# SSD scan of a hybrid decoder step: ScalarE scales the sample states by their decay in place, VectorE adds the products for four batches in one operation

## The reference

```python
def step(s, inp):
    xc, dtc, bc, cc = inp
    acum = jnp.cumsum(dtc * a, axis=1)
    ...
    y_inter = jnp.einsum('bign,bghpn->bighp', cc, s) * jnp.exp(acum)[..., None]
    a_last = acum[:, -1]
    w = jnp.exp(a_last[:, None] - acum) * dtc
    s_new = jnp.exp(a_last)[..., None, None] * s + jnp.einsum('bjgh,bjghp,bjgn->bghpn', w, xc, bc)
```

## Time and profile before

| what | value |
|---|---|
| median of 3 runs | 2334.03 us (2333.56 to 2342.25) |
| the profiled execution | 2328.8 us |
| its span, first to last instruction | 2327.3 us |
| mean granted TensorE clock | 0.955 of full speed |
| PE busy in the span | 2131.6 us, 92% |
| DVE busy | 1436.1 us, 62% |
| ACT busy | 937.9 us, 40% |
| POOL busy | 279.8 us, 12% |
| the states' updates, L2035 on DVE | 256 operations, from 1410.0 to 2048.4 us of the span |

### The profile page before, as it was taken

How to read it: one execution, slowest core, us unless ns; L and a number is a source line. 1 busy time by engine, 2 the same in 40 slices (tenths; PEclk the granted TensorE clock), 3 DMA queues, 4 the chain that set the end, 5 groups by cost and what they waited for, 6 DMA issues and landing times. The chain is left out here.

```text
span 2327.3 us, 41668 instructions
## 1 busy us (share of the span) xinstructions
PE 2131.6 (92%) x15171; PEld 1983.0 (85%) x15171; DVE 1436.1 (62%) x2762; ACT 937.9 (40%) x1260; POOL 279.8 (12%) x423
## 2 busy tenths in 40 slices
PE   6699999999999999968999699999999999749997
PEld 4698989999999898938999698988988988639996
DVE  5553756648465574844434468878878888744433
ACT  3444444434444334313333344544544545423332
POOL 1100201012001010120000102122121131110000
PEclk8799999999999999978999799999999999869999
DMA  4664858577658485547444466566565566336542
GB/s 126 205 174 124 276 159 276 191 226 221 210 158 284 125 281 148 190 174 269 162 156 164 133 175 194 168 194 196 168 218 182 173 200 192 102 143 220 162 154 77
DMA packets 332531, 427.42 MB, mean 184 GB/s; under 512 B 17132, under 2 KB 296220, under 8 KB 330976
## 3 DMA queue, kind: packets, MB, share of 16 engines
q1 hardware_dynamic: 293488, 287.16, 41.0%
q0 software_dynamic: 38720, 138.84, 16.8%
q10 hardware_dynamic: 224, 0.05, 0.0%
HBM read 350.63 MB, written 75.34 MB: 183 GB/s over the span
## 5 line engine op out<-in xcount | busy, mean ns | idle before, releaser
L132 DVE TENSOR_TENSOR w_lo<-w_raw,w_hi 128x1024 fp32r<-128x1024 f32 x512 | 624.9, 1225 | 651.5 <-ACT w_hi L126 641.4
L126 ACT ACTIVATE w_hi<-w_raw 128x1024 fp32r<-128x1024 f32 x512 | 541.4, 1060 | 1017.3 <-PE bank L147 950.4
L145 PE MATMUL bank<-xn_hi,w_hi 128*128 128x288 f32 x3072 | 927.9, 302 | 24.4 <-ACTq L931 12.3
L146 PE MATMUL bank<-xn_lo,w_hi 128*128 128x288 f32 x3072 | 911.7, 297 | 0.0
L147 PE MATMUL bank<-xn_hi,w_lo 128*128 128x288 f32 x3072 | 909.1, 296 | 0.0
L145 PEld LDWEIGHTS bank<-xn_hi,w_hi 128*128 128x128 f32 x3072 | 581.9, 189 | 47.5 <-issue 31.3
L146 PEld LDWEIGHTS bank<-xn_lo,w_hi 128*128 128x128 f32 x3072 | 582.7, 190 | 4.9
L147 PEld LDWEIGHTS bank<-xn_hi,w_lo 128*128 128x128 f32 x3072 | 583.3, 190 | 0.0
L145 PE MATMUL bank<-oc_o_hi,w_hi 128*128 128x288 f32 x512 | 153.9, 301 | 22.9 <-DVE oc_o_lo L1386 21.2
L145 PE MATMUL bank<-oa_o_hi,w_hi 128*128 128x288 f32 x512 | 154.5, 302 | 21.4 <-DVE oa_o_lo L1386 18.5
L146 PE MATMUL bank<-oa_o_lo,w_hi 128*128 128x288 f32 x512 | 153.8, 300 | 0.0
(11 more groups left out here) (439 smaller groups left out, 2358.1 us busy)
## 6 DMA issues: line engine op xcount, KB each, us to landing
w_raw<-in_w_in_ab SPq DMA_DIRECT2D x224, 512.0 KB, 3.9
w_raw<-in_w_in_c SPq DMA_DIRECT2D x128, 512.0 KB, 4.4
w_raw<-in_w_out_ab SPq DMA_DIRECT2D x64, 512.0 KB, 3.4
w_raw<-in_w_out_c SPq DMA_DIRECT2D x64, 512.0 KB, 3.4
state<-in_state_gla POOLq DMA_DIRECT2D x32, 512.0 KB, 10.1
out_gla_s<-state POOLq DMA_DIRECT2D x32, 512.0 KB, 4.3
state<-in_state_mlstm_c POOLq DMA_DIRECT2D x32, 512.0 KB, 9.4
out_mc_s<-state POOLq DMA_DIRECT2D x32, 512.0 KB, 4.7
```

The source lines that it names most:

```text
L126: act.activation(core.w_hi[:, j], core.w_raw[:, j % RAW], ACT.Copy).then_inc(ws["hi"], 1)
L132: dve.tensor_tensor(core.w_lo[:, j], core.w_raw[:, j % RAW], core.w_hi[:, j].bitcast(F32), ALU.subtract).then_inc(ws["split"], 1)
L145: pe.matmul(banks[m][:, 0:T], core.w_hi[:, j, kk, col], hi[:, k], start=f, stop=False)
L146: pe.matmul(banks[m][:, 0:T], core.w_hi[:, j, kk, col], lo[:, k], start=False, stop=False)
```

## The change

ACT now multiplies the old state by its decay, in place, right after it has copied that batch's turned bank: four Copy activations of 128x128 with a per-partition scale from `we`, for each batch, so 32 for a group and 256 in all. A new semaphore `decayed` counts the halves. DVE then needs only an addition, and does it for one product bank at once: one 128x512 `tensor_tensor` in place of four 128x128 `scalar_tensor_tensor`, 64 in all. DVE waits for `decayed` before the first update of a half; ACT waits for the factors (`we_in`) before the first batch.

```diff
-                                 "tails tail_out upd dve act pool_w").split()}
+                                 "tails tail_out upd dve act pool_w decayed").split()}
...
                 act.activation(turned[b % 4], bk[:, :], ACT.Copy).then_inc(free[at(f"st{b}", 0)[0]], 1)
+                if b == 0:
+                    act.wait_ge(s["we_in"], G * 32 + 32)
+                e = TS + TD * b + TD - 1
+                for q in range(4):
+                    ins = act.activation(state[:, b, q], state[:, b, q], ACT.Copy, scale=we[:, q, e:e + 1])
+                if b % 4 == 3:
+                    ins.then_inc(s["decayed"], 1)
...
             bk = wait_full(dve, f"u{i}", G)
-            for b in range(4):
-                S = state[:, 4 * half + b, q]
-                e = TS + TD * (4 * half + b) + TD - 1
-                ins = dve.scalar_tensor_tensor(S, S, we[:, q, e:e + 1], bk[:, b * P:(b + 1) * P], ALU.mult, ALU.add)
-            ins.then_inc(s["upd"], 1)
+            if q == 0:
+                dve.wait_ge(s["decayed"], G * 2 + half + 1)
+            S = state[:, 4 * half:4 * half + 4, q]
+            dve.tensor_tensor(S, S, bk[:].rearrange("p (b n) -> p b n", n=P), ALU.add).then_inc(s["upd"], 1)
             dve.wait_ge(s["upd"], G * 8 + (i + 1))
             dve.sem_inc(free[at(f"u{i}", 0)[0]], 1)
```

## The result

The change makes the kernel faster: 2317.87 us median (2317.16 to 2320.1) against 2334.7 (2333.56 to 2342.25) beside it, a ratio of 0.9923 with a 95% interval of 0.9904 to 0.9941. The forecast was 2329.5, 2323 to 2340, with most of the chance on "no difference that can be told". The profiled executions differ by less, 2328.8 to 2317.5, their spans by 11.7 us.

A forecast was written before the change was run, and what follows sets the result against it. PE paces the kernel, so DVE or ACT time counts only where PE waits. Gains of 3.6 us in seven groups and 0.9 in the last make 4.5: 2334.0 - 4.5 = 2329.5 us, range 2323 to 2340.

The forecast's parts named there:

- no difference that can be told: Whole kernel: a time within 0.5%, about what a measurement can tell from no change; chance 0.78.
- The chain of step 11, and what is in reach: From PE's release at step 11 through copy, split, two updates and `irows` to the y product; only the updates shorten.
- 0.86 us for the shorter pair: DVE at step 11: two updates and the way to `irows` take 1.75 us, not 2.61, in each of seven groups.
- PE is not hurt: Step 7: scalings delay ACT's split of step 8 by 2.27 us, but PE needs it over 10 us later.
- So 0.34 us of the 0.86 is given back, and 0.52 stays: DVE reaches the split of step 11 at 1613.07, where 1612.73 is wanted, because step 7's scalings delay step 8's split.
- the sum's very figure: DVE's way from its split of step 8 to that of step 11, forecast as 10.17 us.
- The last group: Additions save 1.72 us, waiting for ACT's scalings costs 0.8; gain 0.9 us.
- Seven groups: 7 x 0.52 = 3.6 us: Total gain forecast for the seven groups with a projection, 0.52 us each.
- slower, by ScalarE's queue: ACT becomes the bound at step 7 and the last group; loss over 11.7 us from 0.54 us a scaling; chance 0.09.
- The whole wait: DVE's relief removes all PE's `irows` wait, 17.9 us, giving 2316; faster by over 0.5%, with half-way outcomes, has 0.13.

The follow-up runs named there:

- the first-half experiment: The change for batches 0 to 3 alone (steps 2 to 6), the rest as in the kernel before: 2332.13 us, ratio 1.0006 to the kernel before.
- one operation added: Changed kernel plus one unread 128x288 VectorE operation between the updates of step 11 and `irows`: 2324.95 us, ratio 0.997 to the kernel before.
- two operations added after: Changed kernel plus two unread VectorE operations between the updates of step 11 and `irows`: 2331.63 us, ratio 0.9999 to the kernel before.
- one added before: Kernel before plus one unread VectorE operation between the updates of step 11 and `irows`: 2339.04 us, ratio 1.0028.

## Why the prediction was wrong, step by step

- *The chain of step 11, and what is in reach*: right. The wait fell where it was read, and the first-half experiment shows that the updates of steps 5 and 6 don't matter in the loop.
- *0.86 us for the shorter pair*: right. The pair and the way to `irows` took 1.73 us (1612.46 to 1614.19), forecast 1.75, and groups lost 0.88 us. PE's own wait fell by more, 1.96 to 0.96, because 0.14 of it moved to the wait for the bank of u4; "PE is not hurt" by step 7 missed that one.
- *"So 0.34 us of the 0.86 is given back, and 0.52 stays"*: wrong in size. A scaling holds the queue 0.29 us, not 0.314, and the split of step 8 came 1.96 us later against the group's mark (32.62 and 30.66 us behind it), not 2.27. The rows of the changed kernel, DVE's splits of step 8 and 11:

```profile
1601.15 1.23 DVE L132 TENSOR_TENSOR w_lo<-w_raw,w_hi 128x1024 fp32r<-128x1024 f32 x1 [2.91 <-ACT w_hi L126]
...
1611.32 1.22 DVE L132 TENSOR_TENSOR w_lo<-w_raw,w_hi 128x1024 fp32r<-128x1024 f32 x1 [0.34 <-ACT w_hi L126]
```

  From one to the other are 10.17 us, the sum's very figure, but by luck: step 8 to step 9 took 3.52 and not 3.62, and the last part, from the updates to the split, 1.86 and not 1.75, because DVE waited there for ACT's copy, which is still the last to come. That term is 7 x 0.34 = 2.4 us of the miss.
- *The last group*, 0.9 us: measured 1.3 to the end of the kernel. DVE did wait 2.0 us for the scalings there, as forecast, but its second half of updates didn't start 0.8 us later for it: 23.87 us after the group's mark, 23.91 before the change. So the whole 1.72 of the shorter additions came through: the y product comes 28.04 us after the mark and not 29.82, 1.8 sooner, and 0.5 of this is lost behind it.
- *What the sum left out* is the step that failed: it priced a wait of PE at its own length. "Seven groups: 7 x 0.52 = 3.6 us" has no term for TensorE's clock. The page's row of clocks has a digit for 58 us, in which 9 stands for all from 90% up, so a stretch of 3.4 us doesn't show there, and I took the full clock for granted. A window of a few us behind each wait would have shown 0.50 there, and that three of the seven waits cost 1.5 to 3.1 us more than they last. That is 6.1 us in the profiled executions, more than the whole gain that the sum had.
- *The medians* differ by 5.1 us more than the spans. The profiled execution of before, at 2328.8 with three stretches, was faster than all four others beside the changed kernel (2333.56 to 2342.25); without its stretches it would be at 2322.7, and no run of before on any chip got there (the lowest is 2324.55). More stretches in the unprofiled runs would explain both. For those four no clock is on record, but the mean granted clock of the whole program is for the runs beside the experiments. On one chip it averages 0.954 over 20 runs of before and 0.956 over five of the changed kernel. The slowest of the 20 (2345.88 us) has 0.948 and the fastest (2324.55) 0.958, and a line through them falls by 2.2 us for each 0.001; a stretch of 3.4 us that costs 1.5 is 0.0007 of this mean, which makes about 2.1 for 0.001 (an estimate). So the slow runs of before did spend more time at half speed. Where in the program they spent it isn't recorded, so that it was behind the waits for `irows` is argued and not shown. By the same record the traces may not tell all of the shorter waits: the ten runs with one operation added, a wait of 1.49 us, go from 0.958 to 0.952, and the slower ones are the lower ones.
- *The rivals*: slower, by ScalarE's queue, would have needed 0.54 us a scaling; 0.29 was measured. "The whole wait" was wrong as a mechanism, 0.96 us of it is left, and yet its time, 2316, is nearest to what came.

## What to carry to other kernels

When the engine that waits is TensorE, read the granted clock just behind the wait, in windows of 2 or 3 us: here a wait of 1.96 us cost 1.5 to 3.1 us on top of its length in three groups of seven. Before work is moved to another engine to shorten a chain, look whether the result that is waited for must stand behind that work at all; here two state updates stood before it with no need, and swapping the order gave more (20 us) than the change (14 to 17). And follow lateness through the buffers that it holds as well as through the value that it makes: the same 2 us came back through a bank.

## What the runs showed of the hardware

- A wait of TensorE of about 1.96 to 2.47 us in a nearly unbroken stream of matmuls was followed by a stretch at 1.2 GHz in 11 of 28 groups (four traces: before, its first-half variant, two operations added after, one added before). Nine of them began 1.3 to 2.0 us behind the wait's end and lasted 3.4 us. The other two began right at its end and lasted 6.8. With waits up to 1.49 us, and with waits of 0.45, 1.33 and 0.86 one after the other, there was none in 63 groups of nine traces.
- One stretch of 3.4 us cost 1.5 us in this stream.
- A scale read from a column costs ScalarE 0.09 us more than a constant, on 128x128 from SBUF to SBUF: 0.29 us of the queue against 0.20.
